# Feed-forward blocks ordered up, gate, down of the chunk before, with two buffers for the rounded inner features, and the last chunk gated in one piece

## The reference

```python
D_FF = ((8 * D_MODEL // 3) + 127) // 128 * 128      # 2816

def swiglu(h, w1, w3, w2):
    return (jax.nn.silu(h @ w1) * (h @ w3)) @ w2

for l in range(DEPTH):                              # DEPTH = 2
    x = x + 0.5 * swiglu(rmsnorm(x, ffn1_norm[l]), ffn1_w1[l], ffn1_w3[l], ffn1_w2[l])
    ...                                             # mixer, cross attention
    x = x + 0.5 * swiglu(rmsnorm(x, ffn2_norm[l]), ffn2_w1[l], ffn2_w3[l], ffn2_w2[l])
```

## Time and profile before

| | |
|---|---|
| Time, median of 3 runs | 3361.12 us (3351.55, 3361.12, 3370.88) |
| Span of the profiled execution | 3377.2 us |
| PE busy | 3210.1 us, 95% of the span, 18864 matmuls |
| PEld busy | 2834.3 us, 84% |
| DVE busy | 1494.4 us, 44% |
| ACT busy | 1093.0 us, 32% |
| Mean granted TensorE clock over the span | 0.963 |

### The profile page before, as it was taken

How to read it: one execution, slowest core, us unless ns; L and a number is a source line. 1 busy time by engine, 2 the same in 40 slices (tenths; PEclk the granted TensorE clock), 3 DMA queues, 4 the chain that set the end, 5 groups by cost and what they waited for, 6 DMA issues and landing times. The chain is left out here.

```text
span 3377.2 us, 44214 instructions
## 1 busy us (share of the span) xinstructions
PE 3210.1 (95%) x18864; PEld 2834.3 (84%) x18864; DVE 1494.4 (44%) x1752; ACT 1093.0 (32%) x1321; POOL 60.1 (2%) x68
## 2 busy tenths in 40 slices
PE   7999989999979999999999999899999989999998
PEld 7998879898968887988888888788889888888886
DVE  3454443454434445535344444444446353434444
ACT  3433333433332223432333222322225323432222
POOL 0000000000000000010000000000000110000000
PEclk8997998997989999989999999999999999999999
DMA  3111112120222222301322222222223112322222
GB/s 119 64 63 38 59 68 71 39 88 5 71 97 100 97 97 85 120 13 63 105 82 87 89 98 98 77 99 99 87 99 109 42 51 75 107 81 100 90 98 79
DMA packets 41263, 270.99 MB, mean 80 GB/s; under 512 B 6272, under 2 KB 6528, under 8 KB 10016
## 3 DMA queue, kind: packets, MB, share of 16 engines
q1 hardware_dynamic: 41120, 268.99, 22.6%
HBM read 266.81 MB, written 2.10 MB: 80 GB/s over the span
## 5 line engine op out<-in xcount | busy, mean ns | idle before, releaser
L173 DVE TENSOR_TENSOR w_lo<-w_raw,w_hi 128x2048 fp32r<-128x2048 f32 x242 | 554.1, 2290 | 454.1 <-ACT w_hi L167 453.4
L185 PE MATMUL PS<-w_hi,uh 128*128 128x256 f32 x2560 | 734.5, 287 | 12.4 <-DVE ul L329 6.6
L186 PE MATMUL PS<-w_lo,uh 128*128 128x256 f32 x2560 | 727.1, 284 | 0.0
L187 PE MATMUL PS<-w_hi,ul 128*128 128x256 f32 x2560 | 726.9, 284 | 0.0
L167 ACT ACTIVATE w_hi<-w_raw 128x2048 fp32r<-128x2048 f32 x242 | 462.9, 1913 | 637.2 <-PE PS L187 633.3
L185 PE MATMUL PS<-uh,w_hi 128*128 128x512 f32 x1600 | 623.1, 389 | 5.5 <-DVE ul L329 5.5
L186 PE MATMUL PS<-ul,w_hi 128*128 128x512 f32 x1600 | 622.5, 389 | 0.0
L187 PE MATMUL PS<-uh,w_lo 128*128 128x512 f32 x1600 | 622.5, 389 | 0.0
L185 PEld LDWEIGHTS PS<-w_hi,uh 128*128 128x128 f32 x2560 | 494.1, 193 | 24.6 <-issue 15.2
L186 PEld LDWEIGHTS PS<-w_lo,uh 128*128 128x128 f32 x2560 | 494.4, 193 | 1.0 <-issue 1.0
L187 PEld LDWEIGHTS PS<-w_hi,ul 128*128 128x128 f32 x2560 | 494.1, 193 | 0.0
(11 more groups left out here) (280 smaller groups left out, 3219.1 us busy)
## 6 DMA issues: line engine op xcount, KB each, us to landing
w_raw<-in_w SPq DMA_DIRECT2D x242, 1024.0 KB, 4.8
X<-in_x SPq DMA_DIRECT2D x1, 2048.0 KB, 10.1
memory<-in_mem SPq DMA_DIRECT2D x2, 1024.0 KB, 5.0
out<-X SPq DMA_DIRECT2D x4, 512.0 KB, 2.8
bands<-in_bands SPq DMA_DIRECT2D x2, 768.0 KB, 6.0
mask_numbers<-in_masks SPq DMA_DIRECT2D x1, 1152.0 KB, 6.3
p_raw<-in_pT SPq DMA_DIRECT2D x2, 512.0 KB, 6.4
lb<-in_lb_logits SPq DMA_DIRECT2D x2, 512.0 KB, 3.3
```

What stands on the lines that cost most here:

```text
L173: dve.tensor_tensor(self.lo[g % 2][:], self.raw[g % 2][:], self.hi[g % 2][:], ALU.subtract).then_inc(self.lo_done, 1)
L185: pe.matmul(out, sh, mh, start=first, stop=False)
L186: pe.matmul(out, sh, ml, start=False, stop=False)
L187: return pe.matmul(out, sl, mh, start=False, stop=last)
```

## The change

The stream becomes up 0, gate 0, then for each further chunk c: up c, gate c, down c-1, and at the end down 10. All four engines' lists are rewritten for it. `h_hi` and `h_lo` get two buffers each, taken by c % 2; `silu` and `h` keep one. The last chunk is treated like the others. In the down block both products of one bank (k = 0 and 1) now follow each other; before, the two banks of a tile alternated.

```diff
     @block.vector
...
         w.split_lo(dve, g0 + 1)
+        gate(g0 + 1, None, 0, 0)
         w.split_lo(dve, g0 + 2)
-        gate(g0 + 1, None, 0, 1)
+        low(None, 0)
 
         def chunk(i, c):
-            g = g0 + 2 + 3 * c
+            g = g0 + 2 + 3 * (c - 1)
             w.split_lo(dve, g + 1, i, 6)
-            add(g + 1, i, c, 6, (0, 1))
             w.split_lo(dve, g + 2, i, 6)
-            add(g + 1, i, c, 6, (2, 3))
+            gate(g + 1, i, c, 6)
+            add(g + 2, i, c - 1, 6, (0,))
+            low(i, c)
+            add(g + 2, i, c - 1, 6, (1,))
             w.split_lo(dve, g + 3, i, 6)
...
+            add(g + 2, i, c - 1, 6, (2, 3))
...
-        dve.wait_ge(silu_done, NCHUNK)
-        for half in range(2):
-            if half == 0:
-                dve.wait_ge(half_up, LOOPS)
-            else:
-                w.wait_used(dve, END - 2)
-            dve.tensor_tensor(f.h[:, half, :], PS[:, 2 + half, :], f.silu[:, half, :], ALU.mult).then_inc(gated, 1)
-            dve.wait_ge(h_hi, NCHUNK + half)
-            dve.tensor_tensor(f.h_lo[:, half, :], f.h[:, half, :], f.h_hi[:, half, :], ALU.subtract).then_inc(h_lo, 1)
...
     @block.tensor
...
         def down(g, i, c, step):
             w.ready(pe, g, i, step)
-            pe.wait_ge(h_lo, at(i, c))
+            pe.wait_ge(h_lo, at(i, c, 1, 1))
             for t in range(NT):
-                pe.wait_ge(free, at(i, c, NT, t + 1 - NT))
-                down_part(g, t, 0)
-                down_part(g, t, 1).then_inc(summed if t < NT - 1 else w.used, 1)
+                pe.wait_ge(free, at(i, c, NT, t + 1))
+                for half in range(2):
+                    for k in range(2):
...
                 pe.wait_ge(silu_done, at(i, c))
                 up(g, 0, i, 6)
-                down(g + 1, i, c, 6)
                 pe.wait_ge(gated, at(i, c))
-                up(g + 2, 2, i, 6, first_done=half_up if c == 1 else None)
-        w.ready(pe, END - 1)
-
-        for t, k in ((0, 0), (1, 0), (0, 1), (1, 1), (2, 0), (2, 1), (3, 0), (3, 1)):
-            pe.wait_ge(h_lo, NCHUNK + k)
-            if k == 0:
-                pe.wait_ge(free, 2 + NT * (NCHUNK - 1) + t - 1)
-            last = down_part(END - 1, t, k)
...
+                up(g + 1, 2, i, 6)
+                down(g + 2, i, c - 1, 6)
+        down(LAST, None, NCHUNK - 1, 0)
...
-    f.h_hi, f.h_lo = mem.put("h_hi", [P, 2, SEQ], F32R), mem.put("h_lo", [P, 2, SEQ], F32R)
+    f.h_hi, f.h_lo = ([mem.put(f"{n}{i}", [P, 2, SEQ], F32R) for i in range(2)] for n in ("h_hi", "h_lo"))
...
-            order += [up[:, c], down[:, c - 1], gate[:, c]]
+            order += [up[:, c], gate[:, c], down[:, c - 1]]
```

More of the change, by code:

```diff
@@ L998, in ffn_phase @@
     silu_done, gated, h_hi, h_lo = (sem(f"{name}_{n}") for n in ("silu", "gated", "hhi", "hlo"))
-    summed, free, half_up = sem(f"{name}_summed"), sem(f"{name}_free"), sem(f"{name}_halfup")
+    summed, free = sem(f"{name}_summed"), sem(f"{name}_free")
     LOOPS = (NCHUNK - 1) // 2
-    END = g0 + 3 * NCHUNK
+    LAST = g0 + 3 * NCHUNK - 1
+    END = LAST + 1
     def at(i, c, per=1, base=0):
-        return plus(i, 2 * per, per * (1 + c) + base)
+        return plus(i, 2 * per, per * c + base)
     @block.sync
@@ L1018, in _, with silu, chunk @@
     def _(act):
[L1019 to L1026, removed]
-            g = g0 + 2 + 3 * c
-            w.split_hi(act, g + 1, i, 6)
-            w.wait_used(act, g, i, 6)
+        def silu(g, i, step):
+            w.wait_used(act, g, i, step)
             act.activation(f.silu[:], PS[:, 0:2, :], ACT.Silu).then_inc(silu_done, 1)
-            w.split_hi(act, g + 2, i, 6)
-            w.split_hi(act, g + 3, i, 6)
         def high(i, c):
             act.wait_ge(gated, at(i, c, 1, 1))
-            act.activation(f.h_hi[:], f.h[:], ACT.Copy).then_inc(h_hi, 1)
-        with act.Fori(0, LOOPS - 1) as i:
-            for c in range(2):
-                chunk(i, c)
[L1041 to L1044, removed]
-        for half in range(2):
-            act.wait_ge(gated, NCHUNK + half)
-            act.activation(f.h_hi[:, half, :], f.h[:, half, :], ACT.Copy).then_inc(h_hi, 1)
+            act.activation(f.h_hi[c % 2][:], f.h[:], ACT.Copy).then_inc(h_hi, 1)
+        w.split_hi(act, g0 + 1)
+        silu(g0, None, 0)
+        w.split_hi(act, g0 + 2)
+        high(None, 0)
+        def chunk(i, c):
+            g = g0 + 2 + 3 * (c - 1)
+            w.split_hi(act, g + 1, i, 6)
+            silu(g, i, 6)
+            w.split_hi(act, g + 2, i, 6)
+            high(i, c)
+            w.split_hi(act, g + 3, i, 6)
+        with act.Fori(0, LOOPS) as i:
+            for c in (1, 2):
+                chunk(i, c)
         w.split_hi(act, END)
@@ L1061, in _, with gate, low @@
     def _(dve):
-        def gate(g, i, step, n):
-            dve.wait_ge(silu_done, n)
+        def gate(g, i, c, step):
+            dve.wait_ge(silu_done, at(i, c, 1, 1))
             w.wait_used(dve, g, i, step)
             dve.tensor_tensor(f.h[:], PS[:, 2:4, :], f.silu[:], ALU.mult).then_inc(gated, 1)
-            dve.wait_ge(h_hi, n)
-            dve.tensor_tensor(f.h_lo[:], f.h[:], f.h_hi[:], ALU.subtract).then_inc(h_lo, 1)
+        def low(i, c):
+            dve.wait_ge(h_hi, at(i, c, 1, 1))
+            dve.tensor_tensor(f.h_lo[c % 2][:], f.h[:], f.h_hi[c % 2][:], ALU.subtract).then_inc(h_lo, 1)
         def add(g, i, c, step, tiles):
@@ L1072, in add @@
                 if t < NT - 1:
-                    dve.wait_ge(summed, at(i, c, NT - 1, t + 2 - NT))
+                    dve.wait_ge(summed, at(i, c, NT - 1, t + 1))
                 else:
@@ L1080, in _ @@
         w.split_lo(dve, g0 + 1)
+        gate(g0 + 1, None, 0, 0)
         w.split_lo(dve, g0 + 2)
-        gate(g0 + 1, None, 0, 1)
+        low(None, 0)
         def chunk(i, c):
-            g = g0 + 2 + 3 * c
+            g = g0 + 2 + 3 * (c - 1)
             w.split_lo(dve, g + 1, i, 6)
-            add(g + 1, i, c, 6, (0, 1))
             w.split_lo(dve, g + 2, i, 6)
-            add(g + 1, i, c, 6, (2, 3))
+            gate(g + 1, i, c, 6)
+            add(g + 2, i, c - 1, 6, (0,))
+            low(i, c)
+            add(g + 2, i, c - 1, 6, (1,))
             w.split_lo(dve, g + 3, i, 6)
-        with dve.Fori(0, LOOPS - 1) as i:
-            for c in range(2):
+            add(g + 2, i, c - 1, 6, (2, 3))
+        with dve.Fori(0, LOOPS) as i:
+            for c in (1, 2):
                 chunk(i, c)
[L1095 to L1098, removed]
-        dve.wait_ge(silu_done, NCHUNK)
-        for half in range(2):
-            if half == 0:
-                dve.wait_ge(half_up, LOOPS)
-            else:
-                w.wait_used(dve, END - 2)
-            dve.tensor_tensor(f.h[:, half, :], PS[:, 2 + half, :], f.silu[:, half, :], ALU.mult).then_inc(gated, 1)
-            dve.wait_ge(h_hi, NCHUNK + half)
-            dve.tensor_tensor(f.h_lo[:, half, :], f.h[:, half, :], f.h_hi[:, half, :], ALU.subtract).then_inc(h_lo, 1)
-        add(END - 1, None, NCHUNK - 1, 0, (0, 1))
+        add(LAST, None, NCHUNK - 1, 0, (0, 1))
         w.split_lo(dve, END)
-        add(END - 1, None, NCHUNK - 1, 0, (2,))
+        add(LAST, None, NCHUNK - 1, 0, (2,))
         if norm:
             norm.mean(dve, 0, NT - 1)
-        add(END - 1, None, NCHUNK - 1, 0, (NT - 1,))
+        add(LAST, None, NCHUNK - 1, 0, (NT - 1,))
         if norm:
@@ L1118, in _, with up @@
     def _(pe):
-        def up(g, bank, i, step, made=None, first_done=None):
+        def up(g, bank, i, step, made=None):
             w.ready(pe, g, i, step)
[L1121 to L1129, removed]
+            block_to_features(pe, w, g, u, lambda t: PS[:, bank + t, :], made)
         def down(g, i, c, step):
             w.ready(pe, g, i, step)
-            pe.wait_ge(h_lo, at(i, c))
+            pe.wait_ge(h_lo, at(i, c, 1, 1))
             for t in range(NT):
-                pe.wait_ge(free, at(i, c, NT, t + 1 - NT))
-                down_part(g, t, 0)
-                down_part(g, t, 1).then_inc(summed if t < NT - 1 else w.used, 1)
+                pe.wait_ge(free, at(i, c, NT, t + 1))
+                for half in range(2):
+                    for k in range(2):
+                        a = k * D + half * 512
+                        last = split_products(
+                            pe, PS[:, 4 + 2 * (t % 2) + half, :], [x[:, k, t * P:(t + 1) * P] for x in (f.h_hi[c % 2], f.h_lo[c % 2])],
+                            (w.hi[g % 2][:, a:a + 512], w.lo[g % 2][:, a:a + 512]), k == 0, k == 1)
+                last.then_inc(summed if t < NT - 1 else w.used, 1)
         pe.sem_inc(free, 2)
@@ L1142, in _ @@
         with pe.Fori(0, LOOPS) as i:
-            for c in range(2):
-                g = g0 + 2 + 3 * c
+            for c in (1, 2):
+                g = g0 + 2 + 3 * (c - 1)
                 pe.wait_ge(silu_done, at(i, c))
                 up(g, 0, i, 6)
-                down(g + 1, i, c, 6)
                 pe.wait_ge(gated, at(i, c))
```

(12 more changed lines are left out.)

## The result

| | before | after |
|---|---|---|
| Time, median of 4 runs | 3361.23 us (3351.55 to 3370.88) | 3390.39 us (3381.72 to 3397.77) |
| Ratio, with its 95% interval | | 1.0089 (1.0063 to 1.0115) |
| Span of the profiled execution | 3377.2 us | 3390.1 us |
| PE waits for `w_lo` in a feed-forward phase | none | 4, 14.4 us |
| The four phases, first to last matmul, summed | 1441.5 us | 1464.8 us |

The change makes the kernel slower by 0.9%, 29 us by the medians. The forecast was 3382 us, with a range from 3367 to 3398 us.

What follows compares the result with a forecast made beforehand. PE, busy 95%, was taken as the bound, so only phase ends could matter. Late lo weights +15.7, clock +6.0 and ends -0.5 us made +21.2 us on 3361.1: 3382 us, range 3367 to 3398 us.

Steps and rivals of the forecast that it cites:

- The late lo weights: Start of each phase: lo weights queue behind the gate product on DVE, PE enters up 1 3.85 us late.
- The slow first steps: First matmul step after each new wait takes 0.31 us instead of 0.23, costing 0.08 us.
- The clock: Behind each of the four new waits the clock falls for 3.4 us and loses 1.5 us; +6.0 us.
- The reason that the prediction gives for 3.4 us: Shortest earlier low-clock stretch, since dense matmuls follow; the 20.50 us stretch had 86 small matmuls, supposedly sparse.
- 6.8 us each time: Rival: clock low for 6.8 us behind each new wait, +27 us, 3388 us; chance 0.09.
- The rival that the clock stays: Clock does not fall at the new waits: +15.2 us, 3376 us, within 0.5%; chance 0.14.
- The steady chunk: Inside the loop, DVE's added work fits holes between additions, lo weights end at T+9.1 as before; 0 us.
- The rival of a new wait in the loop: Additions and h_lo delay the lo weights beyond 1.9 us of room, every chunk pays: 3420 us; chance 0.05.
- The order of the products: Down blocks: six products in a row per bank instead of three change nothing; 0 us.
- third rival: Down-product order wins back 4.6 us, ends 1.1 us, no clock fall: +10 us, 3371 us; chance 0.06.
- The end: Last down block: PE's small wait goes, 0.27 us won in ffn2 twice, nothing in ffn1; -0.5 us.
- The sum: Whole kernel: 15.7 + 6.0 - 0.5 = +21.2 us, giving 3382 us, slower by 0.63%.

Runs made afterwards that it cites:

- e2: The kernel before with only the lo weights of block g0+2 moved behind the gate product of chunk 0: 3383.2 us, ratio 1.0069 to the kernel before.
- e3: The changed kernel with 16 extra unread matmuls on PE behind gate block 0, filling the wait: 3375.47 us, ratio 1.0044 to the kernel before.
- e7: The changed kernel with 8 extra unread matmuls on PE behind gate block 0, filling half the wait: 3377.43 us, ratio 1.0047 to the kernel before.
- e1: The changed kernel with the lo weights of block g0+2 moved back ahead of the gate product of chunk 0: 3360.44 us, ratio 0.9989 to the kernel before.
- e5: The changed kernel with half of the lo weights of block g0+2 made ahead of the gate product: 3384.16 us, ratio 1.0065 to the kernel before.
- e6: e1 with one buffer each for h_hi and h_lo again, in the new block order: 3371.84 us, ratio 1.0029 to the kernel before.
- e4: e1 with the lo weights of the block behind the phase made one addition earlier in the last down block: 3356.99 us, ratio 0.9997 to the kernel before.

## Why the prediction was right

**The late lo weights.** Forecast: PE restarts 3.85 us late, from four rows of DVE. Measured: 14.63 - 10.88 = 3.75 us in each of the four phases, and 3.75 us again in e2. The 0.1 us too much is the last term, the 0.15 us from DVE's end to the matmul: in the changed trace the lo weights end at 983.52 + 2.28 = 985.80 and PE starts at 985.85, 0.05 us. The slow first steps cost 0.13 us (e3 and e7), forecast as 0.08. e1 and e2 show by taking the line away and adding it alone that it is the cause.

**The clock.** Forecast: it falls at each of the four waits, for 3.4 us, at 1.5 us each. It fell at all four, and at all four of e2. The size was off: it was low for 3.4 us in two phases and for 6.8 us in two, and cost 1.6 and 2.8 us by the difference to e3's up 1. In all 8.9 us and not 6.0. Most of that is the second stretch of 3.4 us in two phases; a little is the price, which was taken from matmuls of 256 columns, 1.8 times as slow at the low clock, while those of 512 columns go from 0.227 to 0.427 us, 1.9 times.

The traces also show what the price depends on. In the two longer falls the low clock began at 1816.45 and 3031.59, 0.8 and 0.7 us before PE's restart, so that part of it lay in the wait and cost nothing; in the two shorter it began 1.2 and 0.5 us behind the restart. A us of low clock in which PE works costs 1 - 0.227 / 0.427 = 0.47 us: that gives 1.6 us for 3.4 us and 2.8 us for 6.8 - 0.8 us. It holds in e2 as well: where the clock fell 1.4 us before the restart and for 6.8 us, up 1 takes 13.53 to 13.56 us, and (6.8 - 1.4) x 0.47 = 2.5 us over 11.0 us is the same. Of the 16 falls behind the new waits in the changed kernel, e2, e5 and e6, the five of 6.8 us began 0.7 to 1.4 us before the restart, and the eleven of 3.4 us between 0.4 us before and 1.2 us behind it. So the length went with how much idle time still lay ahead when the clock fell.

The reason that the prediction gives for 3.4 us doesn't hold: the 86 matmuls in 20.50 us come 0.24 us apart, not at nearly twice the 0.23 us of up 1, and keep PE busy for 19.57 us, so those rows do not set sparse work against dense. And the place of the earlier trace rows, behind which the clock stayed up, has its like in the first layer, where it fell (the row with e7). The forecast kept 6.8 us each time as a rival and as the bound, and the truth lay between the two.

**The rival that the clock stays** fell with the trace. The Trainium skill's example ("TensorE: Matmul & The Clock Gate", section "Seeing it yourself") of a fall 5.2 us after the last matmul is no bound: here the low clock began 3.2 us after the start of the last matmul before the wait (1813.25 to 1816.4, where the step is 3.97 us), and in e2 2.6 us after it (989.57 to 992.13).

**The steady chunk.** Forecast: nothing changes; gate product to T+1.5, `h_lo` to T+5.3, second addition at T+5.69, lo weights from T+6.83 to T+9.1, third addition to T+10.25. With T = 1304.07 the rows say 1.50, 5.31, 5.69, 6.84 to 9.12, and 10.25. The rival of a new wait in the loop falls with the 442 matmuls in 100 us.

**The order of the products.** Forecast: 0, by a block of the first model with the same order. Down blocks take 10.99 us after and 10.98 to 10.99 before. Where the 0.1 us over an up block comes from was not tested; the number of products in a row in one bank is not it. (By rows 3 the excess over 44 blocks is 44 x 0.10 = 4.4 us, not 4.6, which would change the third rival's time by 0.2 us.)

**The end.** Forecast: 0.27 us less in PE's list, kept in `ffn2` and lost in `ffn1`. The stretch from the end of up 1 to the last matmul went from 327.63 to 327.35 us in all four. Behind `ffn1` PE's wait grew from 3.47 to 3.75 us, which takes it back whole, since the last addition (1326.86) again starts without idle time; behind the first layer's `ffn2` it grew by 0.17 us, behind the last not.

**The sum.** The 23.3 us of the phases are the terms above: 4 x 3.75 for the waits, 4 x 0.13 for the first steps, 8.9 for the clock, less 4 x 0.28. In the profiled executions the phases and the steps behind them account for 23.3 + 2 x 0.28 + 0.17 = 24.0 us of loss, 0.71%, against 21.2 forecast; e2, with 24.8 us, was measured at 0.69%. The measured 0.89% has an interval from 0.63 to 1.15% that holds 0.71%; the 5 us between them are no larger than the scatter of the clock elsewhere, and no part of the change explains them.

## What to carry to other kernels

When the order of a stream is rewritten, the prologue needs its own look: the loop here was laid out without a wait, and the loss came from one instruction that was queued behind a product which can't start before its consumer is already waiting. An engine that is busy for 44% of the time still stops the one that is busy for 95% if its list is in the wrong order. Count a wait of the matmul engine at more than its length: behind 2.7 to 3.8 us of idling the clock cost another four to eight tenths of the wait, and matmuls that nobody needs bought that part back (e3, e7). A second buffer for what a loop already hides is only worth what it saves at the loop's ends, which a cheaper trick may already save.

## What the runs showed of the hardware

- The clock fell behind all of the 16 new waits of 2.69 us or more (four each in the changed kernel, e2, e5 and e6), and behind none of the four of 1.94 us in e7.
- The length of a wait alone does not decide. Of 36 other waits with e7's step of 2.17 us the low clock followed 4, and of the 18 steps of 3.16 to 3.75 us behind `ffn1` (two in each trace) it did not follow 3: one each in e2 (3.46 us, at 1334.74), e4 (3.16, at 1304.19) and e6 (3.74, at 2524.28).
- A us at the low clock in which PE worked through matmuls of 128x512 cost 0.47 us; what of the low clock lay in the wait cost nothing.
- A matmul of 128x512 took 0.227 us from start to start at the full clock and 0.427 us at the low one.
- Of the same instructions in the first model, 6480 matmuls, one execution took 972.5 us at a mean clock of 0.92 and another 960.2 us at 0.94. Whole runs of one kernel on one core spread over 40 us (3340.63 to 3380.06, 35 runs of the kernel before).
